# Loading each expert's first weight pair to a spare place and copying it to its own with GpSimd

## What is computed

```
logits = t @ w_router + b_router            # top 4 of 32, softmax gate
h = xb @ w_mlp1[e] + b_mlp1[e]              # 1024 -> 2048
glu, lin = split(h);  glu = min(glu, 7);  lin = clip(lin, -7, 7)
a = glu * sigmoid(1.702 * glu) * (lin + 1)
y = a @ w_mlp2[e] + b_mlp2[e]               # 1024 -> 1024
out[token] += gate * y;   result = rms_norm(h + out, g_final)
```

## Time and profile before

| | us |
|---|---|
| median of 3 runs | 1559.8 (1558.12 to 1562.24) |
| profiled execution | 1561.99 |
| its span | 1560.2 |
| TensorE busy in the span | 1420.2 (91%) |
| VectorE, ScalarE, GpSimd busy | 746.1, 569.1, 331.8 |

### The profile page before, as it was taken

One profiled execution on the slowest core, in us unless ns is written; L12 is line 12 of the kernel. 1 busy time (PEld: TensorE's weight loads), 2 busy tenths in 40 slices (PEclk: granted clock), 3 DMA queues, 4 the chain that ended last, 5 costly groups with the idle time before them and its releaser, 6 DMA issues.

```text
span 1560.2 us, 35409 instructions
## 1 busy us (share of the span) xinstructions
PE 1420.2 (91%) x13321; PEld 759.1 (49%) x13322; DVE 746.1 (48%) x1798; ACT 569.1 (36%) x1081; POOL 331.8 (21%) x220
## 2 busy tenths in 40 slices
PE   6999898899996689999999999999889899999992
PEld 4888676566875234433344434434333443334341
DVE  7999968897206524322333333333323333333237
ACT  4544435654223023323233322432423333223333
POOL 2778786312650000000000000000000000000000
PEclk9999999899998899999999999999999999999996
DMA  4222321111348289999999999999999999999997
GB/s 174 95 95 80 108 81 57 38 42 41 128 155 358 95 324 408 428 429 422 384 372 426 423 428 425 417 428 428 428 427 422 426 419 421 428 396 401 426 417 271
DMA packets 51521, 474.65 MB, mean 304 GB/s; under 512 B 9120, under 2 KB 9376, under 8 KB 26912
## 3 DMA queue, kind: packets, MB, share of 16 engines
q1 hardware_dynamic: 41856, 455.19, 71.0%
q0 software_dynamic: 8480, 16.79, 2.8%
q10 hardware_dynamic: 1152, 2.24, 0.4%
HBM read 471.04 MB, written 16.78 MB: 313 GB/s over the span
## 4 chain that ended last, share of the span: by engine, by line
PE 47%; DMA 17%; issue 2%; DVE 1%; ACT 0%; DVEq 0%; SPq 0%; ACTq 0%; POOLq 0%
PE bank L1141 28%; DMA big<-in_d_w 15%; PE bank L1167 14%; PE bank L1125 1%; PE bank L1153 1%; PE bank L1134 1%; DMA y_rows<-mix,sidx 1%; PE bank L1114 1%; PE bank L1117 0%; ACT mix L1093 0%; DMA xT<-y_rows 0%; DVE xT L1357 0%; DVE uT L1351 0%; DVE uT L1319 0%; ACT xT L1100 0%
## 5 line engine op out<-in xcount | busy, mean ns | idle before, releaser
L1141 PE MATMUL bank<-big,ring 128*32 128x512 f32 x4992 | 570.8, 604 | 41.4 <-DMA big<-in_d_w 22.6
L1141 PEld LDWEIGHTS bank<-big,ring 128*32 128x32 f32 x4992 | 153.1, 111 | 381.5 <-issue 346.9
L1167 PE MATMUL bank<-big,mix 128*32 128x256 f32 x4992 | 288.5, 382 | 2.3 <-DMA big<-in_d_w 2.3
L1167 PEld LDWEIGHTS bank<-big,mix 128*32 128x32 f32 x4992 | 164.8, 110 | 96.8 <-issue 5.8
L1093 ACT ACTIVATE mix<-bank,sgate 32x256 f32<-32x256 f32 x384 | 178.4, 465 | 67.8 <-PE bank L1167 43.0
L1037 POOL DMA_INDIRECT ring<-u_rows,gidx x34 | 34.3, 1009 | 580.8 <-PE bank L1134 567.8
L1081 ACT ACTIVATE ring<-ring 128x256 f32<-128x256 f32 x96 | 40.0, 416 | 313.8 <-DVE ring L1294 313.8
L1078 ACT ACT_TABLE_LOAD x32 | 41.1, 1283 | 260.1 <-PE bank L1125 260.1
L486 PE MATMUL bank<-mix_r,sm_r 128*128 128x512 f32 x304 | 121.7, 400 | 7.4 <-POOL ring_r L242 7.4
L486 PE MATMUL bank<-mix_r,ring_r 128*128 128x512 f32 x320 | 124.6, 390 | 0.0
L486 PE MATMUL bank<-uT_r,sm_r 128*128 128x512 f32 x304 | 118.5, 390 | 0.0
(11 more groups left out here) (281 smaller groups left out, 1772.4 us busy)
## 6 DMA issues: line engine op xcount, KB each, us to landing
big<-in_d_w SPq DMA_DIRECT2D x192, 2048.0 KB, 18.7
ring<-in_d_dense SPq DMA_DIRECT2D x66, 512.0 KB, 3.3
big<-y_rows SPq DMA_DIRECT2D x2, 2048.0 KB, 19.5
xT<-in_d_xT SPq DMA_DIRECT2D x4, 512.0 KB, 5.8
uT<-in_d_x SPq DMA_DIRECT2D x1, 2048.0 KB, 8.5
u_rows<-xT SPq DMA_DIRECT2D x4, 512.0 KB, 17.0
xT<-y_rows SPq DMA_DIRECT2D x1, 2048.0 KB, 12.7
xT<-y_rows SPq DMA_DIRECT2D x4, 512.0 KB, 5.5
```

The costliest lines, as they stand in the source:

```text
L1141: mm = pe.matmul(halves(bank[g][c * G:(c + 1) * G, :], FC), t.xe[:, k, PLACE[g]:PLACE[g] + G], cols, start=(k == 0), stop=(k == KB - 1), t ...
L1167: mm = pe.matmul(bank[PY[g % 2]][c * G:(c + 1) * G, 0:FC], t.aT[:, g, x, b * G:(b + 1) * G], t.w2[:, b, x, c * FC:(c + 1) * FC], start=(b ...
```

## The change

The tile `xT` gets a third use, `t.ahead`, as large as one pair. SP loads pair 0 of every expert but the first there, the others to their places as before. The order of the transfers stays: pair 0 of an expert is issued behind the second half of w2 of the one before. It waits for the end of the copy of the pair before it, in place of TensorE's `s_w1used`. GpSimd copies the pair from `t.ahead` to its own place, 128 partitions of 4096 float32, behind the gather and ahead of the scatter, when it has landed and TensorE has used pair 0 of the expert before; the copy counts up `s_w1[0]`, for which TensorE waits. The last turn of GpSimd's and SP's loops is written out behind them.

```diff
+            def first_pair(i):
+                e = expert_of(sp, i)
+                sp.dma_start(t.ahead[:, :, :], t.d_w1[bass.ds(e, 1), 0].rearrange("e p a n -> (e p) a n")).then_inc(t.s_ahead, 16)
+
+            def others(i, done):
+                e = expert_of(sp, i)
+                for q in range(1, PAIRS):
+                    sp.wait_ge(t.s_w1used, done * PAIRS + (q + 1))
+                    ...
+            first_pair(1)
+            with sp.Fori(0, last - 1) as i:
+                others(i + 1, i)
+                sp.wait_ge(t.s_w1[0], i * 16 + 32)
+                first_pair(i + 2)
+            others(last, ...)
+            sp.wait_ge(t.s_w1[0], last * 16 + 16)
...
+            def serve(i, follows):
                 pool.wait_ge(t.s_gidx, i + 3)
                 pool.wait_ge(t.s_xt, i * 2 + 4)
                 pool.sem_inc(t.s_go, 1)
                 gather()
+                if follows:
+                    pool.wait_ge(t.s_ahead, i * 16 + 16)
+                    pool.wait_ge(t.s_w1used, i * PAIRS + 1)
+                    pool.tensor_copy(t.w1[:, 0:2, :], t.ahead[:, :, :]).then_inc(t.s_w1[0], 16)
                 pool.wait_ge(t.s_ysb, i * NG + NG + 1)
                 ...
+            with pool.Fori(0, last) as i:
+                serve(i, True)
+            serve(last, False)
...
+        t.ahead = halves(xT[:, :], 2 * D)
```

More of the change, by code:

```diff
@@ L1006, in _ @@
             sp.dma_start(t.gfin[:, :], t.d_gfin.partition_broadcast(P)).then_inc(t.s_fin, 16)
-            with sp.Fori(1, n) as i:
+            def first_pair(i):
                 e = expert_of(sp, i)
-                for q in range(PAIRS):
-                    sp.wait_ge(t.s_w1used, i * PAIRS + (q + 1 - PAIRS))
+                sp.dma_start(t.ahead[:, :, :], t.d_w1[bass.ds(e, 1), 0].rearrange("e p a n -> (e p) a n")).then_inc(t.s_ahead, 16)
[3 more added lines that the diff above has]
+                    sp.wait_ge(t.s_w1used, done * PAIRS + (q + 1))
                     sp.dma_start(t.w1[:, 2 * q:2 * q + 2, :], t.d_w1[bass.ds(e, 1), q].rearrange("e p a n -> (e p) a n")).then_inc(t.s_w1[q], 16)
                 for q in range(2):
-                    sp.wait_ge(t.s_w2used, i * 2 + (q - 1))
+                    sp.wait_ge(t.s_w2used, done * 2 + (q + 1))
                     sp.dma_start(t.w2[:, 2 * q:2 * q + 2, :, :],
                                  t.d_w2[bass.ds(e, 1), q].rearrange("e p j a n -> (e p) j a n")).then_inc(t.s_w2[q], 16)
+            first_pair(1)
[3 more added lines that the diff above has]
+                first_pair(i + 2)
+            others(last, sp.value_load(t.lists[0:1, P + 2:P + 3], min_val=E - 2, max_val=E + MORE - 2))
+            sp.wait_ge(t.s_w1[0], last * 16 + 16)
             sp.wait_ge(t.s_scat, last * 16)
@@ L1046, in _ @@
             gather()
-            with pool.Fori(0, n) as i:
+            last = pool.value_load(t.lists[0:1, P + 1:P + 2], min_val=E - 1, max_val=E + MORE - 1)
+            def serve(i, follows):
                 pool.wait_ge(t.s_gidx, i + 3)
@@ L1551, in build @@
         t.s_scat = sem("s_scat")
+        t.s_ahead = sem("s_ahead")
         t.s_x = sem("s_x")
```

## The result

| | before | changed |
|---|---|---|
| median, us | 1560.13 (beside the changed kernel) | 1608.01 (1597.76 to 1613.56, 4 runs) |
| ratio | 1 | 1.0301, 95% interval 1.0278 to 1.0324 |
| profiled execution, its span, us | 1561.99, 1560.2 | 1604.46, 1602.6 |

What follows compares the result with a forecast made beforehand. TensorE paces three-group experts, the DMA two-group ones. On 1559.8 us: VectorE held by the copy +7.7, late first pairs +3.9, start -1.7, last expert's w2 wait -2.0, together +7.9: 1568 us, range 1556 to 1598.

Runs made afterwards that it cites:

- the copy without the place: Kernel before with its own loads, plus a GpSimd copy of `xT` onto itself, 4096 columns, behind the gather; 1617.3 us, ratio 1.0372.

## What to carry to other kernels

When work is put on GpSimd beside VectorE, list every VectorE instruction that runs at the moment the new one starts, not only those that begin under it, and price each by who waits for it: an overlap of 0.04 us cost 4.9 us. A short first piece, or a wait until the last urgent VectorE instruction is done, takes most of such a loss away at once. Not every instruction is held: L1317 and L1330, which read a matmul's result from its bank, ran inside the copy of each three-group expert and kept their 0.68 and 0.42 us; L1319 and L1326, which read and write the tiles `ring` and `mix` alone, did not. And where a kernel alternates between stretches that the DMA and that TensorE paces, sum a loss by stretch: up to the time that TensorE waits for weights it is given back.

## What the hardware showed that was not expected

- **The instruction that began first was the one that was held.** The product's record starts 0.37 to 0.40 us ahead of the copy's, and it is the one that waits, in 11 of 12 cases (17 of 17 in the copy without the place). The Trainium skill (SBUF — State Buffer, "Who interferes with whom") says that a VectorE instruction with two inputs in SBUF contends with a GpSimd instruction that reads SBUF; the trace agrees (L1326 has two such inputs). It also says that issue order decides who blocks; by the recorded starts that is not so here. Nor is the opposite a rule: with half the copy, two products of an empty third group whose records start 0.11 and 0.13 us ahead kept 0.43 us, and there the copies took 2.07 and 2.04 us for 1.90.
- **How much it is held depends on what lies over its end.** All these copies started 0.01 to 0.06 us, mostly 0.05, ahead of the product's normal end. 128 columns: not stretched; 512: by 0.29 us; 2048: by 2.13; 4096: by 3.84. The last two are the copy's columns at 0.83 ns and 0.42 us more (1.71 + 0.42; 3.42 + 0.42), as though the product only began when the copy's stream was over; the first two are less than that. In one expert the copy of 4096 columns began just as far ahead of the product's normal end, and the product kept its time. Timelines of the changed kernel:

```profile
1245.40 0.42 DVE L1326 TENSOR_TENSOR mix<-mix,ring 128x256 f32<-128x256 f32 x1
1245.77 3.61 POOL L1073 COPY big<-xT 128x4096 f32<-128x4096 f32 x1
```

  What decides at the edge is open.
- **GpSimd can be slow beside VectorE too.** Its last scatter took 7.84 us beside eight additions of VectorE in one run, in two kernels, and 1.1 to 2.0 us in the eight kernels where the additions paused after four; no other scatter of the mixture took over 0.95.
- **A wait of 3.1 us was followed by 3.4 us or more at 1.2 GHz in 9 of 11 cases, one of 1.4 us in none of 5.** Between them both are found: the wait of 1.96 us in the kernel before was followed by 3.4 us of it, none of the twelve waits of about 1.9 us in the kernel with the copy behind all products was.
